# Last feed-forward chunk: GpSimd's low parts placed by semaphores beside VectorE's additions, VectorE's work in another order

## The reference

```python
h2 = rms_norm(x, g_ffn[l])
x = x + jnp.square(jax.nn.relu(h2 @ w_ff1[l])) @ w_ff2[l]
```

## Time and profile before

| | us |
|---|---|
| median of 3 runs | 687.33 (685.88, 687.33, 687.7) |
| profiled execution | 684.92 |
| its span | 683.0 |
| busy: TensorE, VectorE, ScalarE, GpSimd | 673.8, 506.5, 368.7, 327.9 |

### The profile page before, as it was taken

How to read it: one execution, slowest core, us unless ns; L and a number is a source line. 1 busy time by engine, 2 the same in 40 slices (tenths; PEclk the granted TensorE clock), 3 DMA queues, 4 the chain that set the end, 5 groups by cost and what they waited for, 6 DMA issues and landing times.

```text
span 683.0 us, 9486 instructions
## 1 busy us (share of the span) xinstructions
PE 673.8 (99%) x3254; PEld 554.9 (81%) x3254; DVE 506.5 (74%) x691; ACT 368.7 (54%) x660; POOL 327.9 (48%) x195
## 2 busy tenths in 40 slices
PE   8999999999999999999999999999999999999977
PEld 6888788888888888888888888888888888888866
DVE  6875798455555456775459879788897978879898
ACT  7764676666666566543357546352554625445350
POOL 1375566455555553444445636245443624635440
PEclk9999999999999999999999999999999999999999
DMA  8223142222322213455222423315123241410203
GB/s 316 93 76 111 53 136 93 79 78 90 97 92 73 70 45 119 162 177 190 84 75 89 141 75 99 116 61 184 61 92 107 77 154 61 148 68 32 92 0 124
DMA packets 22908, 69.86 MB, mean 102 GB/s; under 512 B 2731, under 2 KB 4267, under 8 KB 22876
## 3 DMA queue, kind: packets, MB, share of 16 engines
q1 hardware_dynamic: 22588, 68.92, 30.0%
q10 hardware_dynamic: 288, 0.52, 0.2%
HBM read 67.27 MB, written 2.16 MB: 102 GB/s over the span
## 4 chain that ended last, share of the span: by engine, by line
PE 92%; DVE 6%; DMA 1%; issue 1%; ACT 0%; SPq 0%; DVEq 0%; ACTq 0%
PE bank L1264 21%; PE bank L1266 21%; PE bank L1265 21%; PE bank L1554 6%; PE bank L1556 6%; PE bank L1557 6%; DVE store L1146 3%; PE bank L1408 3%; PE bank L1395 2%; PE bank L1428 1%; PE bank L1430 1%; DVE x_lo L1118 1%; DMA store<-x_t 1%; PE bank L1526 1%; DMA bias_m<-slabs 0%
## 5 line engine op out<-in xcount | busy, mean ns | idle before, releaser
L468 POOL TENSOR_TENSOR w_lo<-w_raw,w_hi 128x1024 fp32r<-128x1024 f32 x79 | 196.0, 2485 | 229.8 <-ACT w_hi L551 229.7
L1264 PE MATMUL bank<-x_hi,w_hi 128*128 128x512 f32 x328 | 132.4, 404 | 0.0
L1266 PE MATMUL bank<-x_hi,w_lo 128*128 128x512 f32 x328 | 128.2, 391 | 0.0
L1265 PE MATMUL bank<-x_lo,w_hi 128*128 128x512 f32 x328 | 127.8, 390 | 0.0
L1264 PE MATMUL bank<-qk_hi,w_hi 128*128 128x512 f32 x320 | 125.0, 391 | 0.0
L1266 PE MATMUL bank<-qk_hi,w_lo 128*128 128x512 f32 x320 | 124.5, 389 | 0.0
L1265 PE MATMUL bank<-qk_lo,w_hi 128*128 128x512 f32 x320 | 124.5, 389 | 0.0
L551 ACT ACTIVATE w_hi<-w_raw 128x1024 fp32r<-128x1024 f32 x80 | 83.8, 1056 | 58.2 <-PE bank L1266 58.2
L1146 DVE SCALAR_TENSOR_TENSOR store<-bank,softmax,store 128x512 f32<-128x512 f32 x101 | 71.8, 742 | 22.6 <-PE bank L1557 22.6
L1554 PE MATMUL bank<-v_parts,x_hi 128*128 128x512 f32 (+1 forms) x218 | 84.7, 388 | 0.3 <-DVE store L1146 0.3
L1557 PE MATMUL bank<-v_parts,x_lo 128*128 128x512 f32 (+1 forms) x218 | 84.4, 387 | 0.0
(11 more groups left out here) (149 smaller groups left out, 1178.5 us busy)
## 6 DMA issues: line engine op xcount, KB each, us to landing
w_raw<-slabs SPq DMA_DIRECT2D x80, 512.0 KB, 3.3
bias_m<-slabs SPq DMA_DIRECT2D x16, 512.0 KB, 3.6
qk_hi_again<-slabs SPq DMA_DIRECT2D x16, 512.0 KB, 5.0
store<-x_t SPq DMA_DIRECT2D x16, 256.0 KB, 4.1
bias_m<-tab_dram SPq DMA_DIRECT2D x8, 256.0 KB, 4.2
out<-store SPq DMA_DIRECT2D x7, 256.0 KB, 2.1
bias_m<-tab_dram SPq DMA_DIRECT2D x8, 128.0 KB, 3.5
w_raw<-slabs ACTq DMA_DIRECT2D x1, 384.0 KB, 4.1
```

The costliest lines, as they stand in the source:

```text
L468: pool.tensor_tensor(w_lo[:, g % WS, :], w_raw[:, g % RAW, :], w_hi[:, g % WS, :].bitcast(F32), ALU.subtract).then_inc(w_lo_ready, lots)
L1264: pe.matmul(out_, wh, xh, start=first, stop=False)
L1265: pe.matmul(out_, wh, xl, start=False, stop=False)
L1266: last = pe.matmul(out_, wl, xh, start=False, stop=end)
```

## The change

In the last chunk only:

- GpSimd does unit 2 ahead of unit 3 and waits three times more: for all four activation sums (`s_ready`) before unit 2, for low part 2 before unit 3, for low part 3 before unit 5. `LAST_B_UNITS` follows.
- ScalarE does down_hi(1) before u_part_hi(4).
- VectorE does down_lo(1) before unit 6's sum; the four additions of products 5 and 6 of chunk 6 in one run, with low parts 1 and 2 behind them and no longer between; low part 3 behind the six additions of product 0, where part 5 was; additions of products 1 and 2 in one run, then down_lo(6) and low parts 5 and 6.

```diff
--- before.py
+++ after.py
@@ -79,7 +79,7 @@
 LAST_UNITS = [0, 3, 1, 2, 4, 5, 6]
 LAST_HALF = 7
 T_UNITS, B_UNITS = (1, 2, 4, 6), (0, 3, 5)
-LAST_T_UNITS, LAST_B_UNITS = (1, 6), (0, 3, 2, 4, 5)
+LAST_T_UNITS, LAST_B_UNITS = (1, 6), (0, 2, 3, 4, 5)
 STEPS = 4 * NH // 2
 
 
@@ -533,8 +533,13 @@
 
                 down_lo(0, c)
                 up_lo(3, c)
-                for k in LAST_B_UNITS[1:]:
-                    down_lo(k, c)
+                pool.wait_ge(s_ready, c * 4 + 4)
+                down_lo(2, c)
+                pool.wait_ge(u_lo_ready, u_count(2, c))
+                down_lo(3, c)
+                down_lo(4, c)
+                pool.wait_ge(u_lo_ready, u_count(3, c))
+                down_lo(5, c)
 
             with pool.Fori(0, CHUNKS - 1) as c:
                 chunk_lows(c)
@@ -805,8 +810,8 @@
                 relu(2, c)
                 square(2, c)
                 u_part_hi(0, c)
+                down_hi(1, c)
                 u_part_hi(4, c)
-                down_hi(1, c)
                 relu(3, c)
                 square(3, c)
                 down_hi(2, c)
@@ -1198,20 +1203,18 @@
                     scaled(j, m, common[m], rest_sum_ready)
 
             u_sums_even(c)
+            down_lo(1, c)
             dve.wait_ge(t_ready, c * 4 + 2)
             dve.wait_ge(b_arrived[B21], c * 16 + 16)
             dve.wait_ge(b_lo_ready, c * 3 + 1)
             dve.tensor_tensor(last_from[6], raw_b[B21], t_2, ALU.subtract).then_inc(t_ready, 1)
-            down_lo(1, c)
             u_sums_odd(c)
             dve.wait_ge(rest_sum_ready, 6)
-            add_product(5, 0, b)
-            add_product(5, 1, b)
+            for k in (5, 6):
+                for m in range(2):
+                    add_product(k, m, b)
             u_part_lo(1, c)
-            add_product(6, 0, b)
             u_part_lo(2, c)
-            add_product(6, 1, b)
-            u_part_lo(3, c)
             dve.wait_ge(sum_read, product_count(6, 1, b))
             for m in range(2):
                 dve.wait_ge(product_done, product_count(0, m, c))
@@ -1219,7 +1222,7 @@
                 scaled(1, m, out_, rest_sum_ready)
                 scaled(3, m, out_, rest_sum_ready)
                 scaled(2, m, out_, sum_read)
-            u_part_lo(5, c)
+            u_part_lo(3, c)
 
             def last_products(k, m, ready):
 
@@ -1227,13 +1230,14 @@
                 scaled(SUM_OF[k], m, bank[BANK_OF[k] + m][:, :], ready)
 
             dve.wait_ge(rest_sum_ready, 10)
-            last_products(1, 0, sum_read)
-            last_products(1, 1, sum_read)
+            for k in (1, 2):
+                for m in range(2):
+                    last_products(k, m, sum_read)
             down_lo(6, c)
+            u_part_lo(5, c)
             u_part_lo(6, c)
-            for k, ready in ((2, sum_read), (3, out_ready)):
-                for m in range(2):
-                    last_products(k, m, ready)
+            for m in range(2):
+                last_products(3, m, out_ready)
             dve.wait_ge(sum_read, product_count(2, 1, c))
             last_products(4, 0, out_ready)
             to, part = sums[2][1], HALVES[1]
```

## The result

The changed kernel takes 680.16 us (median of 4 runs, 680.01 to 680.47), the kernel before beside it 686.61 (4 runs, 685.81 to 687.7): ratio 0.9915, 95% interval 0.990 to 0.993. It is faster, and by more than forecast: 682.4 was predicted, with a range of 681.4 to 684.4. The profiled execution took 680.22 us, span 678.3.

A forecast was written before the change was run, and what follows sets the result against it. VectorE's queue, with GpSimd's timing, was taken to bound the last chunk, costing TensorE 4.98 us of holes. Removing all: 684.92 - 4.98 = 679.94 profiled, 687.33 - 4.98 = 682.4 us median; range 681.4 to 684.4.

The forecast's parts named there:

- The exclusion: Last chunk: GpSimd and VectorE shut each other out when VectorE takes both operands from SBUF, not with one from a bank.
- odd sums' end: VectorE, last chunk: three dependent activation sums were to end near 653.75 instead of 657.83.
- low part 1's end: VectorE, last chunk: was to end at 657.1, with product 1 due at 658.26, so no hole and 1.2 us spare.
- low part 3's end: VectorE, last chunk: held until 662.6, ending at 663.1; product 3 due at 663.70, 0.6 us spare, the smallest margin.
- TensorE's gain: Last chunk: all 4.98 us of holes were to go, 78 starts taking 17.68 us where they took 22.66.
- Rival 2: VectorE's bank additions beside GpSimd are held too: 7.0 us lost against 4.98, 689.3 us, slower; chance 0.04.
- rival 3: The long VectorE times are not GpSimd's and stay with their instructions: 688.5 us, 1.2 slower; chance 0.02.
- rival 1: Thinner margins: odd sums begin at 653.63 as now, or GpSimd's units 3 and 4 take 3.39 each; 683.8 us, chance 0.12.
- rival 4: Something unseen, such as a later bound in VectorE's last eight additions, takes most back: 685.3 to 687.3 us; chance 0.07.
- tail: From TensorE's last start to the span's end, 3.5 us: taken to stay the same last additions and stores.
- GpSimd's 2.85 and 3.42: GpSimd subtraction times beside VectorE, read as GpSimd losing too, against 2.40 us alone.
- the carry to the median: The median shown, 687.33, lies 2.41 above the profiled 684.92; this distance was carried over to the changed kernel.

The follow-up runs named there:

- the first two sets: Two of three groups of follow-up runs, each on its own chip with the kernel before beside it, which took 685.73 us (23 runs) and 685.50 (23).
- e10_unit3_early: The changed kernel without GpSimd's wait for low part 2 ahead of unit 3: 683.02 us (10 runs), 2.8 slower than the changed kernel.

## Why the prediction missed its range though its mechanism held

**The exclusion, and all that follows from it: right.** The trace of after runs 0.62 us late against that of before when chunk 7 begins (up(1) at 634.40 for 633.78). With that added, forecast and trace read: odd sums' end 654.37 and 654.37, low part 1's end 657.7 and 657.71, low part 3's end 663.7 and 663.71, GpSimd's four starts 654.4, 658.4, 660.8, 663.8 and 654.45, 658.40, 660.77, 663.79. TensorE's gain was to be 4.98 and is 22.66 - 17.69 = 4.97. Rival 2 fell at the six bank additions (4.03), rival 3 at s_2 (0.69), rival 1 at the odd sums' start (652.22, where 653.63 + 0.62 would have been unchanged) and the 2.4 us of units 3 and 4, rival 4 at the stream without holes. The price of a wait of GpSimd for VectorE, bounded by 0.15, is 0.08 to 0.09 (s_4 ends at 654.37, unit 2 starts at 654.45). In the profiled pair 4.97 of body and 0.35 of tail, less 0.62 of front, are the 4.70 by which the two moved; that this is near the 4.98 forecast is in part luck, since tail and front were in the sum at nothing.

**GpSimd's 2.85 and 3.42.** I read them as GpSimd losing its turn, and took 2.40 for it alone. In the last chunk that held in every kernel: an instruction that lets no VectorE instruction in first takes 2.34 to 2.45. The 3.39 and 3.42 of the other chunks were not followed up.

**The step that failed: the carry to the median.** "The median shown, 687.33, is 2.41 above, and I carry that over." I took the distance between one execution and the median of three for something both kernels have. It was not. In the 57 executions of the first two sets the kernel before has a median of 685.74, only 0.8 above its profiled execution, so 687.33 was 1.6 too high a start; the changed kernel's profiled execution lay 0.06 above its own median, not 2.41 below. That is 1.6 of the 2.2 us missed.

**Two terms that the sum lacked: the other 0.6.** Between those 57 executions of the kernel before and the 10 of the changed one, the change is worth 685.74 - 680.17 = 5.6 us in the medians and 686.03 - 680.16 = 5.9 in the means. Holes give 4.97. The clock behind the holes: 23 of the 57 have a mean of 0.995 or 0.993, and those at 0.995 took 0.9 more than those at 1.0; 23 x 0.9 / 57 = 0.4 in the mean, if 0.993 is the same fall with one in the front added. Falls in the front don't count, since, counted that way, both kernels have them in about one execution of five (11 of 57, 2 of 10). The tail gives 0.35: the last stores are spread wider, since VectorE now has its first finished sums 1.5 us earlier against its end. Together 5.7, an estimate, since the clock's share stands on means and the tail's on single profiles. I had written that the tail was "the same last additions and stores", and had read from the earlier trace rows that the clock stays at 2.4 GHz, from one execution in which it did.

**The range.** Its width came from the margins of the mechanism, which were good to 0.1 us. The uncertainty lay in the base and was taken as "over 1.8 us" between three runs without asking what makes them differ. A spread of 1.8 in the kernel before, with holes in it, was itself a row to be explained.

What stays open is the front: 649.3 to 651.1 us to the same matmul in thirteen profiled executions that share its code. The three at a clock of 0.87 in their first 10 us are the longest (650.39, 650.65 and 651.13), but the other ten still differ by 1.0. Open too is why a few executions took 2 us more than the rest at a mean clock of 1.0.

## What to carry to other kernels

A GpSimd instruction is cheap beside VectorE work that reads a bank, and costs its whole length beside VectorE work with both operands in SBUF. So place GpSimd by a semaphore at the start of a run of bank additions, and collect those additions into runs; VectorE's order without the placement made things worse. Test each such wait alone: of three, one was worth 2.8 us, one 1.6 to 1.9, one nothing. And carry no distance from one profiled execution to a median: this kernel, with holes in TensorE's stream, paid for them a second time in some of its executions.

## What the runs showed of the hardware

- The clock can fall behind a hole of 2.3 us in otherwise dense matmul work, but not in each execution: the mean of the execution was 0.995 or less in 23 of 57. With a hole of 3.6 us it was 0.995 in 9 of 12 and 0.998 or 0.997 in the rest, with the holes filled below 0.999 in 0 of 12, with holes of 1.0 and 1.7 (`e10_unit3_early`) 1.0 in 10 of 10. At 1.2 GHz a matmul of 512 columns starts 0.427 us after the one before, at 2.4 GHz 0.227.
- GpSimd and VectorE go by turns where VectorE's instruction has both operands in SBUF. With both in waiting, a GpSimd instruction that follows another lets the waiting VectorE instruction in first, 0.45 us for 512 elements, and shows that time in its own duration (2.85 for 2.40). A held VectorE instruction ended 0.54 to 0.56 us after GpSimd's recorded end in all cases read (five in the kernel before, two in the changed one), so GpSimd's recorded ends could be relied on to 0.02 us here, and its durations only where nothing was let in first. The Trainium skill (Perfetto Trace Analysis, "GPSIMD Engine Instruction") counsels against trusting such a span at all; for these subtractions the rows bear that out for the duration and not for the end.
